# A state-space scan's decay exponents: one product with a coarse mask per head, and a triangle applied later

## The chip, the cores and the metric

The kernel runs on one NeuronCore of a Trainium2 chip. The core has a matrix engine (TensorE, "PE" in the rows, with its weight loads as "PEld"), a vector engine (VectorE, "DVE"), a scalar engine (ScalarE, "ACT"), GpSimd ("POOL") and SyncE ("SP"), which issues most transfers. Each engine works through its own list of instructions in order and waits on semaphores for the others. The metric is the device time of one execution in microseconds (us), the median over several runs.

## What is computed

The program is three transformer-like layers on 256 tokens of width 1024. The change lies in the second mixer, a state-space layer (Mamba-2 in chunks). Cut to what matters:

```
def ssd_scan(x, dt, a, bm, cm):            # 32 heads, 4 groups of 8 heads, 2 chunks of 128 tokens
    causal = np.tril(np.ones((L, L), dtype=bool))
    def step(state, inp):
        acs = jnp.cumsum(dt_k * a_g, axis=1)
        seg = acs[:, :, None] - acs[:, None, :]
        lmat = jnp.exp(jnp.where(causal, seg, -jnp.inf))     # 128 x 128 for each head
        cb = jnp.einsum("blgn,bsgn->blsg", c_k, b_k)
        w = cb[..., None] * lmat * dt_k[:, None]
        y = jnp.einsum("blsgh,bsghp->blghp", w, x_k)
        ...                                                  # plus what the state gives, and the new state
```

For each chunk and each head, a 128 x 128 matrix of decays exp(acs[l] - acs[s]) is wanted for tokens s <= l, and zero above. `a` is negative and `dt` positive, so acs falls from token to token: the exponent is at most zero where s <= l, and positive where s > l.

## The kernel before

**Weights.** All weight matrices come as a row of 1 MB chunks. SP loads a chunk into one of three buffers (`raw`); ACT rounds it to a high part (`whi`, L503) and DVE (L510), or POOL for some chunks (L518), subtracts to get the low part (`wlo`). PE multiplies each chunk three times (L522, L523, L524: input high with weight low, and so on). ACT and DVE do a chunk in two pieces of 1024 columns; "a split" below is one such piece.

**The state-space stage.** `pe_ssd_first`, `act_ssd_first` and `dve_ssd_first` make dt, the running sums (`nacs`, minus acs with tokens on partitions) and a transposed copy of the sums in a PSUM bank: 96 rows, three copies of the 32 heads, by 2 x 128 tokens. These sums are cut into three bf16 parts, so that bf16 products add up to them exactly enough: `part[0]` (ACT, L1677), `rest[0]` (DVE, L1705), `part[1]` (ACT, L1683), `rest[1]` (DVE, L1711). Then six products (`spread`, five on POOL at L1730 in `pool_ssd_parts`, one on DVE at L1713) spread them to `segs`, 96 x (2 chunks x 4 heads x 128 tokens) in bf16, with zeros where row and head don't belong together.

**The scan.** For group g (8 heads) and chunk t, `pe_seg` fills two PSUM banks, four heads each ("halves" below, h0 and h1). A half is two bf16 matmuls of 512 columns: identity by the mask `neg_sl` (-1e30 where s > l, L1829), and a one-hot selection `quad` by `segs` (L1831). There are 4 x 2 x 2 = 16 halves. `act_seg` makes E = exp(bank + nacs) by heads (L1842). `pe_ssd_scan` makes cb (L1857) and the transposes of x (L1862); `dve_ssd_scan` multiplies E by cb (L1935, "W"), x by dt (L1939, `xdt`); PE then makes y with E as weights (L1870), the state (L1877), or what the state gives (L1880, "inter"). The second half of a chunk 1 (t = 1) waits for ACT's copy of the state (L1910), and that of a chunk 0 of g > 0 for DVE's `inter` (L1959). At the end of a group y is transposed ("turn", L1891), rounded by ACT (L1925, "high") and reduced by DVE (L1979, "low").

**The order.** While the scan of group g runs, the same engines project the inputs of group g + 1, and at the end the output projection. Strings in `SSD_ORDER` say for each engine which of the streams takes its next step: `a` the scan, `b` the projections (for PE a step is half a chunk, 24 matmuls of 256 columns; later half a chunk of the output projection, 12 of 512), `T` the next split of weights. So the order of the work is fixed by hand on each engine, and an engine that waits holds all that is behind it. Decoded, PE's order around the places that matter is (p1.0a = group 1, projection 0, first half; z = the two projections of z; d0.0 = first step of the output projection):

```
head:  p0.2a p0.2b p0.0a SEG(0,0)h0 p0.0b p0.1a p0.1b SEG(0,0)h1 p1.0a p1.0b p1.1a cb(0,0) p1.1b p1.2a y(0,0) p1.2b state(0)
late:  inter(1) SEG(2,0) p3.0a p3.0b turn(1) ... cb(2,0) p3.2a y(2,0) state(2) p3.2b SEG(2,1) cb(2,1) p3.z0a p3.z0b p3.z1a p3.z1b
       y(2,1) inter(2) SEG(3,0) d0.0 d0.1 turn(2) d1.0 cb(3,0) d1.1 y(3,0) state(3) SEG(3,1) d2.0 d2.1 cb(3,1) d3.0 y(3,1)
```

A projection into a PSUM bank waits until DVE has taken the earlier content: p1.0a waits for the third convolution tap (L1577) of projection (0,0), p1.1a for that of (0,1), and d0.0 for DVE's product with z (L1800) after ACT's tanh of it.

Of the kernel before, what the change touches and what calls it, by code (L numbers as in the profile page):

```python
# [120 lines left out]
def _host_neg():  # L121
# [5 lines left out]
    out = [np.where(c > r, n, z), np.where(r > c, n, z), np.where(r % 64 <= np.arange(64)[None, :], z, n)]  # L127
# [4 lines left out]
    out.append(((a[:, None] // 4 % 8 == np.arange(8)[None, :]) & (a[:, None] < 96)).astype(np.float32))  # L132
    out.append((a[:, None] % 4 == np.arange(4)[None, :]).astype(np.float32))
# [126 lines left out]
def build(nc, wall, x_d, mem_d, cols_d, rows_d, masks_d, neg_d, out_d):  # L260
# [19 lines left out]
    with root:  # L280
# [32 lines left out]
        negf_w = 2 * 128 + 64 + 30 + 8 + 4 + 1  # L313
# [19 lines left out]
        neg_qk, neg_sl, neg_gd = negb[:, 0:128], negb[:, 128:256], negb[:, 256:320]  # L333
        quad, fourth = negb[0:96, 350:358], negb[0:96, 358:362]
# [1331 lines left out]

        def act_ssd_first(e, split):
            e.wait_ge(*at("srow", "galog"))
            e.activation(Am[:, :], srow[:, 32:64], ACTF.Exp).then_inc(*up("act.ssd", "A"))
            e.wait_ge(*at("pe.proj", C_DT))  # L1670
# [6 lines left out]
            e.activation(part[0], banks[7][0:96, 0:256], ACTF.Copy).then_inc(*up("act.ssd", "part", 0))  # L1677
# [5 lines left out]
            e.activation(part[1], rest[0], ACTF.Copy).then_inc(*up("act.ssd", "part", 1))  # L1683

        def dve_ssd_first(e, split):
# [19 lines left out]
            e.tensor_tensor(rest[0], banks[7][0:96, 0:256], part[0], SUB).then_inc(*up("dve.ssd", "rest", 0))  # L1705
# [5 lines left out]
            e.tensor_tensor(rest[1], rest[0], part[1], SUB).then_inc(*up("dve.ssd", "rest", 1))  # L1711
            e.wait_ge(*at("dve.ssd", "rest", 1))
            e.tensor_tensor(*spread(rest[1], 0, 2), MUL).then_inc(*up("dve.ssd", "segs"))  # L1713

        def spread(v, t, i):

            rows = slice(32 * i, 32 * i + 32)
            return (segs[rows, t, :, :], tl(v[rows, :], t).unsqueeze(1).to_broadcast([32, 4, 128]),
                    bc(fourth[rows, :], 128))

        def pool_ssd_parts(e):
            for t in range(2):
                for i, v in enumerate((part[0], part[1], rest[1])):
                    if (t, i) == (0, 2):
                        continue
                    if i == 2:
                        e.wait_ge(*at("dve.ssd", "rest", 1))
                    else:
                        e.wait_ge(*at("act.ssd", "part", i))
                    e.tensor_tensor(*spread(v, t, i), MUL).then_inc(*up("pool.ssd", "segs", t, i))  # L1730
                    e.wait_ge(*at("pool.ssd", "segs", t, i))
# [82 lines left out]
        def pe_seg(e, g, t):  # L1814

            for b2 in range(2):
# [6 lines left out]
                if t == 0:  # L1823
                    e.wait_ge(*at("pool.ssd", "segs", 0, 1))
                    e.wait_ge(*at("dve.ssd", "segs"))
                else:
# [68 lines left out]
        def act_ssd_scan(e, g):  # L1895
# [1207 lines left out]
```

## Time and profile before

| | us |
|---|---|
| median of 3 runs | 1207.2 (1207.15 to 1210.69) |
| the profiled execution | 1207.32 |
| its span in the trace | 1205.5 |
| PE busy | 1179.6 (98%) |
| DVE busy | 847.9 (70%) |
| ACT busy | 651.6 (54%) |
| POOL busy | 151.9 (13%) |

Busy time is the sum of an engine's instructions over the span. The state-space stage takes the span from about 360 to 560 us. A profile is read by stages: an average of 98% on PE can hide stretches in which PE stands still, and only there do the other engines set the time. Matmuls are pipelined: a row's duration is longer than the step from one start to the next, and the step is what a matmul costs in a stream.

### The profile page before, as it was taken

The page shows a single profiled execution, that of the slowest core. Times are in us where ns is not written, and L with a number is a line of the kernel's source. Part 1 is how long each engine was busy: PE and PEld are TensorE (multiplying, and loading weights), DVE is VectorE, ACT ScalarE, POOL GpSimd, SP SyncE. Part 2 cuts the span into 40 slices and gives each one's busy share as a digit, 9 for nine tenths or more (in the row PEclk, how much of TensorE's full clock was granted, in tenths as well). Part 3 has the DMA queues.
Part 4 walks back from the last instruction along what each step waited for, and adds up shares of the span by engine and source line. Part 5 has one row for each costly group of instructions (what it writes and reads, how often), then busy time and mean ns, then how long its engine had stood idle before and what let it go on. Part 6 is the DMA issues. An engine that isn't in the chain of part 4 may idle for free.

```text
span 1205.5 us, 23231 instructions
## 1 busy us (share of the span) xinstructions
PE 1179.6 (98%) x9876; PEld 1078.4 (89%) x9876; DVE 847.9 (70%) x1299; ACT 651.6 (54%) x1171; POOL 151.9 (13%) x143
## 2 busy tenths in 40 slices
PE   8999999999999999999999999999999999999998
PEld 8897789999889898978999988999989878999986
DVE  6677777888557988886788874857567776655542
ACT  4657556666446665645666653665434534644431
POOL 1320000000002332101000000103443311000000
PEclk9999999999999999999999999999999999999999
DMA  8832226565635443352755564452322322755540
GB/s 295 280 141 88 89 101 211 195 210 191 233 106 172 152 184 141 114 183 105 257 194 183 207 244 157 178 175 105 105 108 71 111 102 90 278 192 193 182 168 35
DMA packets 31623, 196.68 MB, mean 163 GB/s; under 512 B 4000, under 2 KB 5664, under 8 KB 9376
## 3 DMA queue, kind: packets, MB, share of 16 engines
q1 hardware_dynamic: 27504, 185.17, 43.3%
q10 hardware_dynamic: 4016, 10.03, 2.6%
q8 instruction: 78, 1.28, 0.4%
q14 instruction: 25, 0.20, 0.0%
HBM read 193.09 MB, written 1.05 MB: 161 GB/s over the span
## 4 chain that ended last, share of the span: by engine, by line
PE 85%; DVE 6%; ACT 4%; issue 2%; POOL 1%; DMA 1%; ACTq 1%; DVEq 0%; POOLq 0%
PE bank L522 24%; PE bank L524 23%; PE bank L523 23%; DVE wlo L510 2%; ACT whi L503 1%; PE bank L1870 1%; PE bank L1108 1%; PE bank L1165 1%; PE bank L1192 1%; PE bank L2514 1%; PE bank L702 1%; DMA raw<-in_wall 1%; PE bank L2457 1%; ACTq L973 1%; PE bank L2981 1%
## 5 line engine op out<-in xcount | busy, mean ns | idle before, releaser
L510 DVE TENSOR_TENSOR wlo<-raw,whi 128x1024 fp32r<-128x1024 f32 (+1 forms) x325 | 390.2, 1238 | 90.7 <-ACT whi L503 90.0
L522 PE MATMUL bank<-xT,wlo 128*128 128x256 f32 (+1 forms) x1512 | 425.5, 281 | 4.3 <-DVE wlo L510 2.2
L523 PE MATMUL bank<-xT,whi 128*128 128x256 f32 (+1 forms) x1512 | 419.9, 278 | 0.0
L524 PE MATMUL bank<-xT,whi 128*128 128x256 f32 (+1 forms) x1512 | 419.9, 278 | 0.0
L503 ACT ACTIVATE whi<-raw 128x1024 fp32r<-128x1024 f32 (+1 forms) x349 | 349.4, 1048 | 116.1 <-PE bank L524 86.5
L522 PEld LDWEIGHTS bank<-xT,wlo 128*128 128x128 f32 (+1 forms) x1512 | 282.2, 187 | 8.8 <-DVE xc L1577 2.8
L523 PEld LDWEIGHTS bank<-xT,whi 128*128 128x128 f32 (+1 forms) x1512 | 282.2, 187 | 0.9 <-issue 0.5
L524 PEld LDWEIGHTS bank<-xT,whi 128*128 128x128 f32 (+1 forms) x1512 | 282.0, 187 | 0.2
L644 POOL TENSOR_TENSOR rr<-rr,nhalf 128x1 f32<-128x1 f32 x34 | 24.8, 729 | 709.7 <-DVE rr L632 522.3
L522 PE MATMUL bank<-whi,gT 128*128 128x512 f32 x264 | 104.6, 396 | 0.0
L524 PE MATMUL bank<-whi,gT 128*128 128x512 f32 x264 | 104.4, 395 | 0.0
L523 PE MATMUL bank<-wlo,gT 128*128 128x512 f32 x264 | 104.3, 395 | 0.0
L522 PE MATMUL bank<-whi,xT 128*128 128x256 f32 (+1 forms) x320 | 96.0, 300 | 2.5 <-DVE xT L718 2.5
L523 PE MATMUL bank<-wlo,xT 128*128 128x256 f32 (+1 forms) x320 | 93.0, 291 | 0.0
L524 PE MATMUL bank<-whi,xT 128*128 128x256 f32 (+1 forms) x320 | 93.0, 291 | 0.0
L518 POOL TENSOR_TENSOR wlo<-raw,whi 128x1024 fp32r<-128x1024 f32 x24 | 61.3, 2559 | 120.2 <-ACT whi L503 111.5
L522 PEld LDWEIGHTS bank<-whi,xT 128*128 128x128 f32 x320 | 60.4, 189 | 7.4 <-DVE xT L718 2.8
L523 PEld LDWEIGHTS bank<-wlo,xT 128*128 128x128 f32 x320 | 60.4, 189 | 1.8 <-issue 0.5
L524 PEld LDWEIGHTS bank<-whi,xT 128*128 128x128 f32 x320 | 60.3, 188 | 1.4
L524 PEld LDWEIGHTS bank<-whi,gT 128*128 128x128 f32 x264 | 49.6, 188 | 11.9
L523 PEld LDWEIGHTS bank<-wlo,gT 128*128 128x128 f32 x264 | 49.6, 188 | 11.7
L522 PEld LDWEIGHTS bank<-whi,gT 128*128 128x128 f32 x264 | 49.6, 188 | 11.6
(383 smaller groups left out, 1747.3 us busy)
## 6 DMA issues: line engine op xcount, KB each, us to landing
raw<-in_wall SPq DMA_DIRECT2D x173, 1024.0 KB, 4.9
grow<-in_rows ACTq DMA_DIRECT2D x13, 512.0 KB, 5.8
h<-in_x SPq DMA_DIRECT2D x4, 256.0 KB, 5.1
dsk<-in_rows ACTq DMA_DIRECT2D x4, 256.0 KB, 3.5
memx<-in_mem ACTq DMA_DIRECT2D x1, 1024.0 KB, 12.1
out<-h SPq DMA_DIRECT2D x4, 256.0 KB, 2.3
masks<-in_masks SPq DMA_DIRECT2D x1, 580.0 KB, 13.4
D<-Tx ACTq DMA_DIRECT2D x4, 128.0 KB, 5.9
```

Of the source, the lines that this page charges most:

```text
L503: e.activation(whi[i % NHL][:, o:o + w], raw[i % NRAW][:, o:o + w], ACTF.Copy).then_inc(*up("act.high", p))
L510: e.tensor_tensor(wlo[i % NHL][:, o:o + w], raw[i % NRAW][:, o:o + w], whi[i % NHL][:, o:o + w], SUB).then_inc(*up("dve.low", p))
L518: e.tensor_tensor(wlo[i % NHL][:, o:o + w], raw[i % NRAW][:, o:o + w], whi[i % NHL][:, o:o + w], SUB).then_inc(*up("pool.low", p))
L522: e.matmul(out, a[1], b[0], start=start, stop=False)
L523: e.matmul(out, a[0], b[1], start=False, stop=False)
L524: return e.matmul(out, a[0], b[0], start=False, stop=stop)
L644: return e.tensor_tensor(v, v, nhalf[:, :].to_broadcast([128, n]), ALU.pow)
L702: r = e.transpose(tl(turn_bank(k, t, n), j), tl(xs_of(k, t), c), ident)
L973: e.dma_start(D2[kv][64 * l2:64 * l2 + 64, par::2, 0:256 - l2], T[kv][64 * par:64 * par + 64, :, l2:256]).then_inc(*up(f"shift{kv}", par, ...
L1108: r = e.matmul(tl(wbank(2 * m + p), i * (t + 1) + kb), qT[rows, 4 * (g // 2) + h0 + i, 128 * t:128 * t + 128], tl(kz[br][rows, g // 2, :], ...
L1165: r = e.transpose(tl(wbank(n), kb * k + i), tl(aP[place(n)], i * (W // 128) + kb), ident)
L1192: r = e.matmul(banks[6 + g // 2][64 * p:64 * p + 64, 128 * h0:128 * h0 + 128 * k], vv[br][:, kb, 64 * (g + p):64 * (g + p) + 64], aPT[(2 * ...
```

## The change

The mask and the selection go into one product. The bf16 parts of the sums stay where they are, 96 rows `parts` by 2 x 128 tokens, and the 32 rows below hold `fours`: 1 where the column's token belongs to the row's block of four tokens. The weights of a head, `pick`, hold a one-hot of the head in rows 0 to 95 and, in the 32 rows below, `later`: -1e30 where the token's block of four is later than the row's. One matmul of 128 x 128 by 128 columns then gives acs[l], and -1e30 where s lies in a later block of four than l. Within a block of four, tokens s > l are not masked: their exp is over 1. So W takes the smaller of E and 1, and multiplies by a cb that has been multiplied by a triangle of ones and zeros (`tri`).

- PE: a half is four matmuls of 128 columns in place of two of 512.
- POOL: `pool_ssd_parts` is gone. DVE: its `spread` is gone, the rests take 64 and 32 rows instead of 96.
- DVE: eight products of cb by `tri` (128 x 128 in PSUM) are new, in front of W, which becomes a scalar_tensor_tensor.
- ACT: `fours`, `later` and `pick` of group 0 ahead of dt, `pick` of the next group in each of groups 0 to 2.
- The orders of all four engines are new. PE's, decoded at the same places:

```
head:  p0.2a p0.2b p0.0a p0.0b SEG(0,0)h0 p0.1a p0.1b SEG(0,0)h1 p1.0a p1.0b p1.1a cb(0,0) p1.1b p1.2a p1.2b y(0,0) state(0)
late:  inter(1) p3.0a SEG(2,0) p3.0b turn(1) ... cb(2,0) p3.2a y(2,0) state(2) SEG(2,1) cb(2,1) p3.2b p3.z0a p3.z0b
       y(2,1) inter(2) SEG(3,0) p3.z1a p3.z1b turn(2) d0.0 cb(3,0) d0.1 y(3,0) state(3) d1.0 SEG(3,1) d1.1 cb(3,1) d2.0 d2.1 y(3,1)
```

DVE's new order has one split in place of two between the convolution of (0,2) and the first tap of (0,0), and the other after that tap.

The diff, cut:

```diff
@@ _host_neg
-    out = [np.where(c > r, n, z), np.where(r > c, n, z), np.where(r % 64 <= np.arange(64)[None, :], z, n)]
+    fours = np.where(r < 32, np.where(c // 4 == r, 1, z), np.where((r >= 96) & (c // 4 > r - 96), n, z))
+    out = [np.where(c > r, n, z), fours, np.where(r % 64 <= np.arange(64)[None, :], z, n)]
...
@@ build
-        neg_qk, neg_sl, neg_gd = negb[:, 0:128], negb[:, 128:256], negb[:, 256:320]
-        quad, fourth = negb[0:96, 350:358], negb[0:96, 358:362]
+        neg_qk, neg_gd = negb[:, 0:128], negb[:, 256:320]
+        fours, later, head1 = negb[0:32, 128:256], negb[96:128, 128:256], negb[0:96, 350:382]
...
-        segs = sb([96, 2, 4, 128], bf16, sst, "segs")
+        pick = sb([128, 8, 128], bf16, sst, "pick")
...
-        part = [stT[0:96, 128 * i:128 * i + 128].bitcast(bf16) for i in range(2)]
-        rest = [yy[1][0:96, 256 * i:256 * i + 256] for i in range(2)]
+        parts = cols[:, _COLS["fc0"][0]:_COLS["fc0"][0] + 128].bitcast(bf16)
+        rest = yy[1][0:64, 0:256]
...
+        def act_pick(e, g):
+
+            e.activation(pick[0:96, :, :], bc(head1[:, 8 * g:8 * g + 8], 128), ACTF.Copy).then_inc(*up("act.scan", "pick", g))
...
@@ act_ssd_first
             e.activation(Am[:, :], srow[:, 32:64], ACTF.Exp).then_inc(*up("act.ssd", "A"))
+            e.activation(parts[96:128, :].rearrange("p (t n) -> p t n", t=2), fours.unsqueeze(1).to_broadcast([32, 2, 128]),
+                         ACTF.Copy).then_inc(*up("act.ssd", "fours"))
+            e.activation(pick[96:128, :, :], later.unsqueeze(1).to_broadcast([32, 8, 128]), ACTF.Copy).then_inc(
+                *up("act.ssd", "later"))
+            act_pick(e, 0)
             e.wait_ge(*at("pe.proj", C_DT))
...
-            e.activation(part[0], banks[7][0:96, 0:256], ACTF.Copy).then_inc(*up("act.ssd", "part", 0))
+            e.activation(parts[0:96, :], banks[7][0:96, 0:256], ACTF.Copy).then_inc(*up("act.ssd", "part", 0))
...
-            e.activation(part[1], rest[0], ACTF.Copy).then_inc(*up("act.ssd", "part", 1))
+            e.activation(parts[0:64, :], rest, ACTF.Copy).then_inc(*up("act.ssd", "part", 1))
@@ dve_ssd_first
-            e.tensor_tensor(rest[0], banks[7][0:96, 0:256], part[0], SUB).then_inc(*up("dve.ssd", "rest", 0))
+            e.tensor_tensor(rest, banks[7][0:64, 0:256], parts[0:64, :], SUB).then_inc(*up("dve.ssd", "rest", 0))
...
-            e.tensor_tensor(rest[1], rest[0], part[1], SUB).then_inc(*up("dve.ssd", "rest", 1))
-            e.wait_ge(*at("dve.ssd", "rest", 1))
-            e.tensor_tensor(*spread(rest[1], 0, 2), MUL).then_inc(*up("dve.ssd", "segs"))
-        def spread(v, t, i):
-...
-        def pool_ssd_parts(e):
-...
+            e.tensor_tensor(parts[32:64, :], rest[32:64, :], parts[32:64, :], SUB).then_inc(*up("dve.ssd", "rest", 1))
@@ pe_seg
                 if t == 0:
-                    e.wait_ge(*at("pool.ssd", "segs", 0, 1))
-                    e.wait_ge(*at("dve.ssd", "segs"))
-                else:
-                    e.wait_ge(*at("pool.ssd", "segs", 1, 2))
-                q = 2 * g + b2
-                e.matmul(bv[:, :].rearrange("p (i n) -> p i n", i=4), identb[:, :],
-                         neg_sl.unsqueeze(1).to_broadcast([128, 4, 128]), start=True, stop=False)
-                e.matmul(bv[:, :], quad[:, q:q + 1].to_broadcast([96, 128]), segs[:, t, :, :].rearrange("p i n -> p (i n)"),
-                         start=False, stop=True).then_inc(*up("pe.scan", "seg", g, t, b2))
+                    e.wait_ge(*at("act.scan", "pick", g))
+                if (g, t) == (0, 0):
+                    e.wait_ge(*at("act.ssd", "later"))
+                    e.wait_ge(*at("act.ssd", "fours"))
+                    e.wait_ge(*at("dve.ssd", "rest", 1))
+                for i in range(4):
+                    r = e.matmul(tl(bv, i), pick[:, 4 * b2 + i, :], tl(parts, t), start=True, stop=True)
+                r.then_inc(*up("pe.scan", "seg", g, t, b2))
@@ act_ssd_scan
                 yield
+                if t and g < 3:
+                    act_pick(e, g + 1)
...
@@ dve_ssd_scan
-                e.wait_ge(*at("act.scan", "seg", g, t, 1))
-                e.wait_ge(*at("pe.scan", "cb", g, t))
-                e.tensor_tensor(E[:, :, :], E[:, :, :], banks[6][:, 0:128].unsqueeze(1).to_broadcast([128, 8, 128]),
-                                MUL).then_inc(*up("dve.scan", "w", g, t))
+
+                e.wait_ge(*at("pe.scan", "cb", g, t))
+                e.tensor_tensor(banks[6][:, 0:128], banks[6][:, 0:128], tri, MUL).then_inc(*up("dve.scan", "cb", g, t))
+                e.wait_ge(*at("act.scan", "seg", g, t, 1))
+                e.wait_ge(*at("dve.scan", "cb", g, t))
+                e.scalar_tensor_tensor(E[:, :, :], E[:, :, :], 1.0, banks[6][:, 0:128].unsqueeze(1).to_broadcast([128, 8, 128]),
+                                       ALU.min, MUL).then_inc(*up("dve.scan", "w", g, t))
...
@@ SSD_ORDER
             "pe": (
-                "bbbbbbbabbbbbbbabbbbbbbbbbbaabbbbbbababbbbbaaaaabbbaabaabbbbbbaaaabbbbbbaabaabbbbbaabaaabbaaaabbaaaabbbb"
...
+                "bbbbbbbbabbbbbbabbbbbbbbbbbaabbbbbbbaabbbbbaabaaabbaabaabbbbbbaaaabbbbbbaabaabbbbbaabbaaabaabaabaaaabbbb"
...
@@ gpsimd
             split.to(C_S + 4)
-            pool_ssd_parts(e)
```

## Rows read from the trace of the kernel before

**Rows 1.** The chain that ended last: shares of the span by engine.
```profile
PE 85%; DVE 6%; ACT 4%; issue 2%; POOL 1%; DMA 1%; ACTq 1%; DVEq 0%; POOLq 0%
```

**Rows 2.** Busy time by stretches: start:end, length, then each engine's busy us (instructions).
```profile
375.00:390.00 15.00, 13.93 (x114) 13.57 (x115) 13.83 (x19) 10.24 (x16) 7.42 (x5) 1.00 0.68 223
390.00:405.00 15.00, 12.89 (x105) 12.15 (x105) 12.88 (x22) 10.68 (x22) 3.05 (x1) 1.00 0.55 198
...
420.00:440.00 20.00, 20.00 (x164) 18.67 (x163) 16.93 (x24) 13.62 (x31) 3.36 (x5) 1.00 0.39 143
```

**Rows 3.** PE's timeline, 385 to 413: start, duration, form, [idle before, releaser].
```profile
388.10 0.36 PE L522 MATMUL bank<-xT,wlo 128*128 128x256 f32 x1 [0.27 <-DVE wlo L510]
396.35 0.39 PE L522 MATMUL bank<-xT,wlo 128*128 128x256 f32 x1 [1.91 <-DVE xc L1577]
402.47 0.39 PE L522 MATMUL bank<-xT,wlo 128*128 128x256 f32 x1 [0.20 <-DVE xc L1577]
412.17 0.33 PE L1867 MATMUL bank<-masks,bcn 128*128 128x128 f32 x1 [0.29 <-DVE E L1935]
412.77 2.00 PE L1870 MATMUL bank<-xdt,E 128*128 128x64 f32 x16 [0.27 <-DVE xdt L1939]
```

**Rows 4.** PE's timeline: two halves of the exponents and what follows.
```profile
420.98 0.39 PE L1829 MATMUL bank<-negb,identb 128*128 128x512 bf16 x1
...
421.87 0.38 PE L1857 MATMUL bank<-bcn 128*128 128x128 f32 x2
```

**Rows 5.** Weight loads of one half; and eight bf16 matmuls of 350 columns in a row.
```profile
420.98 0.10 PEld L1829 LDWEIGHTS bank<-negb,identb 128*128 128x128 bf16 x1
420.99 0.10 PEld L1831 LDWEIGHTS bank<-segs,negb 96*128 96x128 bf16 x1
...
362.27 1.35 PE L761 MATMUL bank<-negb,identb 128*128 128x350 bf16 x8
```

**Rows 6.** DVE's timeline, 377 to 390, and POOL's instructions that run beside it.
```profile
377.19 2.36 DVE L510 TENSOR_TENSOR wlo<-raw,whi 128x1024 fp32r<-128x1024 f32 x2 [0.26 <-ACT whi L503]
379.82 0.41 DVE L1705 TENSOR_TENSOR yy<-bank,stT 96x256 f32<-96x256 f32 x1
...
381.41 1.13 DVE L1711 TENSOR_TENSOR yy<-yy,stT 96x256 f32<-96x256 f32 x1
382.57 1.41 DVE L1713 TENSOR_TENSOR segs<-yy,negb 32x512 bf16<-32x512 f32 x1
384.02 3.94 DVE L510 TENSOR_TENSOR wlo<-raw,whi 128x1024 fp32r<-128x1024 f32 x2
387.88 2.42 DVE L1577 SCALAR_TENSOR_TENSOR bcn<-bank,cols,bcn 128x255 f32<-128x255 f32 x6
...
381.22 3.67 POOL L1730 TENSOR_TENSOR segs<-stT,negb 32x512 bf16<-32x512 bf16 x3 [0.78 <-ACT stT L1683]
```

**Rows 7.** PE's timeline: late waits of PE in the scan.
```profile
472.00 0.39 PE L1829 MATMUL bank<-negb,identb 128*128 128x512 bf16 x1 [0.31 <-DVE xs L1959]
520.88 0.46 PE L1857 MATMUL bank<-bcn 128*128 128x128 f32 x2 [0.30 <-DVE yT L1979]
528.00 0.39 PE L1829 MATMUL bank<-negb,identb 128*128 128x512 bf16 x1 [0.21 <-ACT stT L1910]
```

**Rows 8.** ACT's copy for dt, and PE's instruction that waits for it.
```profile
366.44 0.37 ACT L1671 ACTIVATE xs<-bank 32x256 f32<-32x256 f32 x1 [1.78 <-PE bank L524]
...
369.16 0.63 PE L571 MATMUL bank<-masks,xs 32*128 32x32 f32 x4
```

**Rows 9.** Groups by line and shape, 370 to 550: busy us, mean ns of one, idle before.
```profile
L503 ACT ACTIVATE whi<-raw 128x1024 fp32r<-128x1024 f32 x53 | 54.0, 1063 | 4.8 <-PE bank L524 3.2 <-DMA raw<-in_wall 1.4
L1935 DVE TENSOR_TENSOR E<-E,bank 128x1024 f32<-128x1024 f32 x8 | 9.7, 1217 | 2.0 <-PE bank L1857 2.0
L1979 DVE SCALAR_TENSOR_TENSOR yT<-bank,cols,yT 128x128 fp32r<-128x128 f32 x32 | 8.6, 344 | 3.0 <-ACT yT L1925 3.0
L1800 DVE SCALAR_TENSOR_TENSOR zs<-zs,bank 128x512 f32<-128x512 f32 x8 | 5.5, 686 | 5.4 <-ACT zs L1775 5.4
```

More of the change, by code:

```diff
@@ L130, in _host_neg @@
         out.append(np.where(16 * cc + 31 <= a[:, None] + 128 * t, z, n))
-    out.append(((a[:, None] // 4 % 8 == np.arange(8)[None, :]) & (a[:, None] < 96)).astype(np.float32))
-    out.append((a[:, None] % 4 == np.arange(4)[None, :]).astype(np.float32))
+    out.append(((a[:, None] % 32 == np.arange(32)[None, :]) & (a[:, None] < 96)).astype(np.float32))
     out.append((a[:, None] >= 31).astype(np.float32))
@@ L312, in build @@
         masks = sb([128, _MASKS], name="masks")
-        negf_w = 2 * 128 + 64 + 30 + 8 + 4 + 1
+        negf_w = 2 * 128 + 64 + 30 + 32 + 1
         negb = sb([128, negf_w - 1], bf16, name="negb")
@@ L1710, in dve_ssd_first @@
             e.wait_ge(*at("act.ssd", "part", 1))
-            e.tensor_tensor(rest[1], rest[0], part[1], SUB).then_inc(*up("dve.ssd", "rest", 1))
-            e.wait_ge(*at("dve.ssd", "rest", 1))
-            e.tensor_tensor(*spread(rest[1], 0, 2), MUL).then_inc(*up("dve.ssd", "segs"))
-        def spread(v, t, i):
-            rows = slice(32 * i, 32 * i + 32)
-            return (segs[rows, t, :, :], tl(v[rows, :], t).unsqueeze(1).to_broadcast([32, 4, 128]),
-                    bc(fourth[rows, :], 128))
-        def pool_ssd_parts(e):
[L1722 to L1727, printed above, removed]
-                    else:
-                        e.wait_ge(*at("act.ssd", "part", i))
-                    e.tensor_tensor(*spread(v, t, i), MUL).then_inc(*up("pool.ssd", "segs", t, i))
-                    e.wait_ge(*at("pool.ssd", "segs", t, i))
+            e.tensor_tensor(parts[32:64, :], rest[32:64, :], parts[32:64, :], SUB).then_inc(*up("dve.ssd", "rest", 1))
         def pe_ssd_proj(e, g):
@@ L1908, in act_ssd_scan @@
                     e.wait_ge(*at("pe.scan", "state", g))
-                    e.wait_ge(*(at("pe.scan", "inter", g - 1) if g else at("pool.ssd", "segs", 1, 2)))
+                    if g:
+                        e.wait_ge(*at("pe.scan", "inter", g - 1))
                     e.activation(stT[:, :], banks[5][:, :], ACTF.Copy).then_inc(*up("act.scan", "state", g))
@@ L1943, in dve_ssd_scan @@
                     e.wait_ge(*at("pe.scan", "turn", g - 1, t))
-                elif t:
-                    e.wait_ge(*at("pool.ssd", "segs", 1, 2))
                 e.tensor_tensor(yy[t][:, :], banks[7][:, :], dsk[:, :], MUL).then_inc(*up("dve.scan", "skip", g, t))
@@ L2763, in build @@
             "pe": (
[L2764 to L2765 removed]
+                "bbbbbbbbabbbbbbabbbbbbbbbbbaabbbbbbbaabbbbbaabaaabbaabaabbbbbbaaaabbbbbbaabaabbbbbaabbaaabaabaabaaaabbbb"
+                "bbaabbbbbaaaaaaabbbbbbbaaaabbaaaabbaabaabaabaaabbbaabbbbaaaabbTTTTTTTTTTTTTTTTTTTTTTTTTTTTTTTTTTTTTTTTTT"
                 "TTTTTTTT"),
             "act": (
[L2768 to L2769 removed]
+                "TTbbbTbbbTbbbTaTbbbbbbTTabbbTbbbbbbTTbbbaaTTaTabbbbbbTaaaabbbbbTTbbaaTTTaaaaabbbaabbbTbbbaaTTTaabbbbbbaa"
+                "aabbbTaabbTTbbTaaaaabbbTaaaabbbTTTTbbbaTaaaaabbbaaTbbbTaaaaabbbbbbbaaTTTaaTaaTaaaaTTTTaaaaaTTTaaTTbbbbbb"
                 "bbbbbbbb"),
             "dve": (
[L2772 to L2773 removed]
+                "TTbbbbbbTbbbbTbbTTbbbbbbTTbbbbbbaaaabbbbTTTababTbbbbaaabbaaabbbbTTTaTTTTaaaTbbbbaababaaabbbbbabaaabbbbbT"
+                "TTbaaTbbbbaaTTTaaaTbbbbaabbaTTTaaaTabbbbTaaabbaaaTbbbbabaaaTbaabbbbaTaaaTaTaaaTTTTaaTaTaaTTaaTTaTTbbbbbb"
                 "bbbbbbbb"),
             "pool": (
[L2776 removed]
+                "TTTTTTTTTTTTTTaaaaaaaaaaTTTaaaaaaaTTTTTaaaaaaaaaaTTTTaaaaaaaTTTTaaaaaaaaaaaaaaaaaaaaaaaaaaaaaaaaTTTTTTTT"
                 "TTTTTTTTTTTTaa"),
```

7 lines of the change are left out of this document (removed).

## The prediction

> **What bounds the kernel now.** I read the chain of work that ended last first: PE carries 85% of the span [rows 1]. So a microsecond taken from PE's stream is worth nearly a microsecond, and other engines count only where PE stands still. The busy times by stretches say where that is [rows 2]: from 420 us on PE is busy 20.00 of 20.00 us, but only 13.93 of 15.00 from 375 and 12.89 of 15.00 from 390, where the scan starts. There DVE is busy 13.83 and 12.88. PE's timeline names what ended each pause there: DVE every time, 0.27, 1.91, 0.20, 0.29 and 0.27 us, 2.94 together [rows 3]. A restart after a pause also shows its first matmul longer than its neighbours and starts late in the stream, by about 0.16 us each (a row's end lies about that much behind the start of the next one in a stream); with five restarts the pauses cost some 3.7 us. DVE's list tells why it is late: between 381 and 388 it does the two last steps of the three-part cut (1.13 and 1.41) and a pair of weight splits that takes 3.94, while POOL runs its spreads; a like pair took 2.36 shortly before [rows 6]. So the change touches two things that set the time: PE's own columns, and DVE's lateness at the head.
>
> **Term A, the matmuls.** A half goes from two matmuls of 512 columns to four of 128. Two halves in the trace take 0.89 us from the start of the first to the start of the next work [rows 4]: 0.445 a half. For the new ones the trace has bf16 matmuls of 350 columns with a weight load each: eight in 1.35, the last one lasting about 0.31, so 1.04 / 7 = 0.149 each [rows 5]; by columns 128 would take 0.054. I take 0.057, so 0.23 a half, a gain of 0.215, and 16 x 0.215 = 3.4 us. What speaks against it is that there are now four weight loads where there were two. A load's row lasts 0.10 us, longer than 128 columns. But two loads start 0.01 us apart [rows 5], so most of that row is latency that the next load overlaps. Bounds: a load that takes its whole row, 4 x 0.098 = 0.39 a half, leaves 16 x 0.055 = 0.9 us; loads that are hidden without any overhead give 16 x (0.445 - 0.214) = 3.7. I am near the upper end, because the pair of loads in row 5 is the same kind of load.
>
> The Trainium skill ("TensorE: Matmul & The Clock Gate", section "Back-to-back issue gap") gives about 81 ns for each 128-column matmul in a stream of load and matmul pairs. By that figure (an estimate from the page) a half takes 0.32, the term is 16 x 0.12 = 1.9, and the kernel comes out at 1202.8. No row here has bf16 matmuls of just 128 columns, so the trace neither agrees nor disagrees.
>
> **Term B, the head.** DVE loses the spread (1.41), and without POOL's spreads beside it I take the last cut at the 0.41 of the first one, 0.7 less, and the pair of splits at 2.36, 1.6 less [rows 6]. Together 3.7: DVE begins the convolution of (0,2) at about 384.3 instead of 388. Follow PE: before, p0.0b let go at 388.10 - 0.27 - 0.16 = 387.67 [rows 3]; a half that is 0.215 shorter makes it 387.45, the splits of p0.1 are long done, so the 0.27 pause goes. p0.1 takes 396.35 - 2.07 - 0.445 - 388.10 = 5.7 us [rows 3], to 393.1, and the second half ends at 393.3. p1.0a then waits for the third tap of (0,0). With the new order DVE does the six taps of (0,2) in 2.4 [rows 6] to 386.75, its silu, one split, the first tap at about 389.3 (PE's p0.0b and ACT's 1 us come before), a second split, and the other taps to about 392.9. PE need not wait: 393.3 instead of 396.35. p1.1a needs the taps of (0,1), by the same counting at 398.9 against PE's 399.0, a tie. y(0,0) now has one projection step more in front (p1.2b, half of 5.7), which covers W. So all five pauses could go, 3.7 us. I take the first two in full (2.18 + 0.32 = 2.5) and half of the other three (0.6), because the tie can tip: 3.1 us. Bounds: 0, if a weight transfer or ACT holds PE there instead, and 3.7.
>
> **Term C, the new order later on.** SEG(2,0) now has a projection step in front of it, and the 0.31 pause for DVE goes (0.47 in the stream); SEG(3,1) likewise, 0.21 (0.37) [rows 7]. But SEG(2,1) now stands right behind state(2), as SEG(3,1) did before, and pays that 0.37 plus the 0.2 by which its first half has become shorter; SEG(3,0), which still stands right behind inter(2), hides 0.2 less. And d0.0, now right behind p3.z1b and turn(2), must wait until ACT has made the tanh of z (half of an L503 piece, 0.53) and DVE the product (0.69) [rows 9]; the transposes of the turn cover most of that, about 0.7 stays open (0.3 to 1.2); turn's rounding is then covered by d0.0, and the 0.30 pause of cb(3,0) [rows 7] mostly goes. In sum +0.84 - 0.57 - 0.2 - 0.7 + 0.2, about -0.5 us, bounds -1.5 and +0.5.
>
> **What I cost at nothing.** ACT's `fours`, `later` and `pick` of group 0 stand in front of the copy for dt: one short and two of 1024 columns, about 0.4 + 2 x 1.06 by L503 [rows 9] = 2.5. ACT waits there for 1.78 us anyway, so dt comes 0.7 later, at 367.5; its only reader on PE starts at 369.16 [rows 8]. If that cover were gone it would cost 0.7. The three later picks, 1.06 each, lie where ACT waits for PE; behind them are queued tanhs and splits, and PE's next halves need them only a group later. Should one fall in front of a late exp, it costs 1.06. cb by `tri`, eight times, is like L1979 (0.344) [rows 9]. DVE now waits for cb before it waits for E; behind it are queued W, xdt and the splits. Where cb comes long before E it is hidden; where cb comes last (after the "low" of the last group), W ends 0.35 later, and y has a step of 2.8 us in front of it, of which W and xdt used 1.9. W itself as scalar_tensor_tensor stays as it is: L1800 is of that kind and takes 0.686 for 512 columns, L1935 1.217 for 1024 [rows 9]. A dearer W is bounded by twice that, but no row speaks for it. The transfers of weights follow DVE's splits, which come earlier.
>
> **Sum.** 3.4 + 3.1 - 0.5 = 6.0 us. The profiled execution took 1207.32 (span 1205.5 and 1.8 around it), and the median of the runs is 1207.2, 0.1 from it: 1207.3 - 6.0 = 1201.3 us.
>
> **Rivals.** (1) *The head stays as late as it is.* Term B is 0: PE stands at p1.0a or p1.1a for something that was hidden behind DVE, a transfer or the chain PE, ACT, DVE through one bank and its three taps. For it: the tie at p1.1a. Against it: every pause in rows 3 names DVE, and DVE is 92% busy there. Time: 1207.3 - 3.4 + 0.5 = 1204.4. (2) *The weight loads show.* Term A is 0.9: 1207.3 - 0.9 - 3.1 + 0.5 = 1203.8. For it: the load's 0.10 us row against 0.054 of columns; against it: loads 0.01 apart. (3) *Both*: 1206.9. (4) *Slower: DVE becomes the bound in the scan.* The places are cb to y of (1,0), (1,1), (2,0) and (3,0), where PE now has a single step, 2.8 us, between them. DVE's chain there is 0.35 + 1.22 + 0.69 = 2.3 from cb. It decides once DVE reaches cb more than 0.5 late; DVE is busy 16.93 of 20 [rows 2] and the new order puts splits (1.2 each) between. Two splits late, 2.4, costs 1.9 at each of the four, 7.6 in all: 1207.3 - 6.0 + 7.6 = 1208.9. Against it: PE had pauses of at most 0.5 there before, and the splits can be counted in the order: at most one stands directly ahead.
>
> **How the numbers follow.** The forecast has 0.55 (1199.9 to 1203.2 by the bounds of A, B and C that I think likely), rival 1 0.17, rival 2 0.12, rival 3 0.07, rival 4 0.09. The predicted time is the forecast's. The range must leave out no more than 2 in 10: it runs from 1199.8 (A and B at their upper ends, C at zero: 1207.3 - 3.7 - 3.7 = 1199.9) to 1206.6, which takes in rivals 1 and 2 and leaves out 3 and 4 and a little below. A measurement of this kernel can tell about 0.3%, 3.6 us, from no change, so "faster" is below 1203.6 and "slower" above 1210.8: faster is the forecast, half of rival 2 and a little of rival 1, 0.63; slower is the upper half of rival 4, 0.06; the same is the rest, 0.31.
>
> **What would show it.** In the profile of the changed kernel: a half's four matmuls 0.05 to 0.06 apart and the next work 0.23 behind the first (A; 0.32 or 0.39 means that loads show). The pair of splits behind the cut at 2.4 instead of 3.94, no pause of PE above 0.5 us between 376 and 415, and p1.0a at about 393 instead of 396.35 (B). A pause of 0.4 to 1.2 in front of d0.0, and one of about 0.6 between the halves of SEG(2,1) (C). ACT's copy for dt at about 367 with PE's turn of it unmoved. Wrong would be: pauses in front of y that name E or xdt, or PE waiting for weights at the head.

## The result and the profile after

The changed kernel takes 1228.2 us (median of 4 runs, 1227.0 to 1229.6) against 1207.3 of the kernel before, measured beside it: a ratio of 1.0171, interval 1.0155 to 1.0186. The forecast was 1201.3 and its range ended at 1206.6, so it was wrong by its sign. The profiled execution took 1227.2, with a span of 1225.1 against 1205.5.

The page of the changed kernel, busy time by engine, and the shares of the chain that ended last (before in [rows 1]):

```profile
PE 1200.4 (98%) x9908; PEld 1103.1 (90%) x9908; DVE 845.7 (69%) x1306; ACT 657.5 (54%) x1177; POOL 141.4 (12%) x138
...
PE 90%; DVE 5%; ACT 2%; issue 2%; POOL 1%; DMA 0%; DVEq 0%; POOLq 0%; ACTq 0%
```

PE's share of the chain has grown from 85% to 90%, and its busy time by 20.8 us. So the time isn't in a new wait; PE's own instructions have become slower. The stretch that the change aimed at looks as forecast at first sight (busy time by stretches, columns as in [rows 2]; the same work stands some 7 us later than before, dt's turn at 376.32 instead of 369.16):

```profile
375.00:390.00 15.00, 14.25 (x118) 13.86 (x117) 9.26 (x18) 10.57 (x16) 0.00 (x0) 1.00 0.44 151
390.00:405.00 15.00, 15.00 (x131) 14.91 (x130) 13.58 (x24) 12.09 (x23) 0.00 (x0) 1.00 0.67 241
420.00:440.00 20.00, 19.59 (x161) 18.48 (x161) 17.27 (x29) 14.02 (x25) 7.70 (x5) 1.00 0.40 155
```

From 390 PE is busy 15.00 of 15.00; before, with the work 7 us earlier, it was 12.89 [rows 2]. So I went through the trace by stages, from the start of one known product to that of another. In the rows xT is the transposed input of a projection, gT the transposed inner values of a feed-forward block and yT the transposed result of the state-space layer, each kept as a high and a low part. The up-projection of the first feed-forward block, from the last turn of its norm (L825, L827 after) to the first product with gT, before and then after:

```profile
188.71 0.60 PE L825 MATMUL bank<-masks,xs 128*128 128x128 f32 x4
...
292.51 0.40 PE L522 MATMUL bank<-whi,gT 128*128 128x512 f32 x1
```
```profile
189.49 0.60 PE L827 MATMUL bank<-masks,xs 128*128 128x128 f32 x4
...
299.36 0.40 PE L524 MATMUL bank<-whi,gT 128*128 128x512 f32 x1
```

That is 103.80 before and 109.87 after, in code that the change doesn't touch. The state-space stage, from the turn of dt (369.16, [rows 8]) to the last product with yT, got shorter. Its end before, then its start and end after:

```profile
566.80 0.39 PE L524 MATMUL bank<-whi,yT 128*128 128x512 f32 x1
```
```profile
376.32 0.29 PE L573 MATMUL bank<-masks,xs 32*128 32x32 f32 x1
...
571.16 0.39 PE L526 MATMUL bank<-whi,yT 128*128 128x512 f32 x1
```

197.64 has become 194.84. All stages, worked out in this way, make up the difference of the spans:

| stage | before, us | after, us | difference |
|---|---|---|---|
| up to the first up-projection | 188.71 | 189.49 | +0.8 |
| three up-projections | 103.8 each | 109.87 each | +18.2 |
| state-space stage | 197.64 | 194.84 | -2.8 |
| between the second and the third (memory, third mixer, a down-projection) | 342.78 | 345.50 | +2.7 |
| all the rest | | | +0.6 |
| span | 1205.5 | 1225.1 | +19.5 |

Within an up-projection PE never pauses. Windows of PE alone (length, PE busy, instructions, granted clock, DMA share, GB/s), the same 50 us before and then after:

```profile
200.00:250.00 50.00, 50.00 (x443) 1.00 0.59 203
```
```profile
200.00:250.00 50.00, 50.00 (x419) 1.00 0.60 208
```

The clock is full in both, and the transfers bring as much. But 443 products have become 419 (each count has some two that only reach into the window). From start to start, over the products that begin in it, a step takes 113.3 ns before and 120.0 after. A product's own row still lasts 0.28; only the step to the next one has grown.

### The profile page after: what moved, and what is told of

It is laid out like the page before. It is cut to its first block, busy times and chain, and to the rows that moved or that the text cites. A ratio compares the mean times of both kernels' runs of the same rounds, so it can differ in the third digit from the quotient of the medians.

```text
span 1225.1 us, 23298 instructions
## 1 busy us (share of the span) xinstructions
PE 1200.4 (98%) x9908; PEld 1103.1 (90%) x9908; DVE 845.7 (69%) x1306; ACT 657.5 (54%) x1177; POOL 141.4 (12%) x138
## 3 DMA queue, kind: packets, MB, share of 16 engines
HBM read 193.10 MB, written 1.05 MB: 158 GB/s over the span
## 4 chain that ended last, share of the span: by engine, by line
PE 90%; DVE 5%; ACT 2%; issue 2%; POOL 1%; DMA 0%; DVEq 0%; POOLq 0%; ACTq 0%
PE bank L524 25%; PE bank L526 24%; PE bank L525 24%; DVE wlo L512 2%; PE bank L1110 1%; PE bank L1860 1%; PE bank L1167 1%; PE bank L1194 1%; PE bank L704 1%; DVE xc L1579 1%; ACT whi L505 1%; PE bank L2508 1%; PE bank L2451 1%; PE bank L2974 0%; DVE xT L720 0%
## 5 line engine op out<-in xcount | busy, mean ns | idle before, releaser
L524 PE MATMUL bank<-xT,wlo 128*128 128x256 f32 (+1 forms) x1512 | 432.1, 286 | 1.6 <-DVE wlo L512 1.6
L526 PE MATMUL bank<-xT,whi 128*128 128x256 f32 (+1 forms) x1512 | 427.7, 283 | 0.0
L525 PE MATMUL bank<-xT,whi 128*128 128x256 f32 (+1 forms) x1512 | 424.9, 281 | 0.0
```

Of the source, the lines that this page charges most:

```text
L524: e.matmul(out, a[1], b[0], start=start, stop=False)
L525: e.matmul(out, a[0], b[1], start=False, stop=False)
L526: return e.matmul(out, a[0], b[0], start=False, stop=stop)
```

## The experiments

Two theories. **P**: the step depends on where the operands lie. The wider mask (`negf_w`, 363 to 383 columns) makes `negb` longer, and every tensor allocated behind it moves by 32 bytes on each partition: xT from 128960 to 128992, gT, yT and the rest alike. **Q**: the instructions of the change cost the time. Unused bytes in the allocation part the two. Addresses below are the program's own; "distance" is that of xT from `whi` and `wlo`, beyond a multiple of 256 bytes: 64 before, 96 after.

**Moved without the change, changed without the move.** The four edits, in this order: the changed kernel with 32 bytes more (all behind `negb` 64 further than before), the kernel before with the 32 bytes of the change, with 32 in front of xT and 32 behind it, and with 64.

```
  e1, behind negb (changed kernel):  +  sb([128, 8], name="pad")
  e2, behind negb (kernel before):   +  sb([128, 8], name="pad")
  e3, ahead of and behind xT:        +  sb([128, 8], name="pad")   (twice)
  e4, behind negb (kernel before):   +  sb([128, 16], name="pad")
```

> The changed kernel with 32 unused bytes behind the mask tensor, so that every tensor behind it starts at a multiple of 64 bytes again. Theory P (place in memory: the wider mask tensor moved xT and all behind it by 32 bytes, and TensorE's products that read xT became slower): each up-projection takes 103.8 us again instead of 109.9, matmul steps 113 ns instead of 119 to 122, and the kernel comes out at 1202 to 1204, since the state-space stage alone had become 2.8 us shorter. Theory Q (the change itself costs the 21 us, by another way than memory): 1226 to 1230 as before the padding.

> The kernel before with 32 unused bytes behind the mask tensor and nothing else: its tensors get the addresses that they have in the changed kernel. Theory P: 1207.3 + 3 x 6.07 for the three up-projections + about 4 for the other products of xT = 1229 to 1232. Theory Q: 1207, no change.

> The kernel before with 32 unused bytes in front of xT and 32 behind it: only xT lies 32 bytes off a multiple of 64, all else stands at multiples of 64. Theory P with xT as the one operand that matters: as when all is shifted, 1229 to 1232. Rival P2 (the products are slowed by another of the shifted tensors, or by the engines that read and write the others): 1207 to 1212. Theory Q: 1207.

> The kernel before with 64 unused bytes behind the mask tensor: all addresses behind it are those of the changed kernel with its padding, at multiples of 64 (xT at a multiple of 512 instead of 64 only). Theory P with 64 bytes as what counts: 1207, no change. Rival P3 (a coarser multiple counts too): 1203 or less. Theory Q: 1207.

| run | xT's distance | us | ratio to before | products in 50 us, by up-projection |
|---|---|---|---|---|
| e1, changed | 128 | 1220.5 | 1.0095 [1.0071, 1.0119] | 424, 424, 424 |
| e2, before | 96 | 1231.5 | 1.0189 [1.0163, 1.0215] | 419, 419, 419 |
| e3, before | 96 | 1226.3 | 1.0145 [1.0123, 1.0167] | 419, 419, 419 |
| e4, before | 128 | 1222.8 | 1.0118 [1.0096, 1.0141] | 419, 424, 419 |

The window from 200 to 250 us in e2 (443 products before, 419 in the changed kernel):

```profile
200.00:250.00 50.00, 50.00 (x419) 1.00 0.59 208
```

The kernel before, not changed in any instruction, loses 24 us by 32 unused bytes, and its count falls to that of the changed kernel. Q falls. At the same addresses the changed kernel is the faster one: 1228.2 against 1231.5 (e2), and 1220.5 (e1) against 1222.8 (e4). What also fell is the first form of P, that a multiple of 64 bytes mends it: e1 and e4 lie on one and are still slow. e3 and e2 differ by 5 us with xT at the same place and the same counts, so other tensors' places count too. And in e4 the stages of one execution differ: at 128 a stage goes at 120.0 ns or at 118.7.

**Which distance.** e5 is the changed kernel with `nhalf` in a spare column of `valid`, so that h, xT and all behind them get their old addresses; e6 and e8 move by 128; e7 moves raw, whi and wlo along with xT.

```
  e5:  -  valid = sb([128, 2], name="valid")
       +  valid3 = sb([128, 3], name="valid")
       +  valid = valid3[:, 0:2]
       -  nhalf = sb([128, 1], name="nhalf")
       +  nhalf = valid3[:, 2:3]
  e6, behind negb (changed kernel):  +  sb([128, 24], name="pad")
  e7, ahead of raw (kernel before):  +  sb([128, 16], name="pad")
  e8, behind negb (kernel before):   +  sb([128, 32], name="pad")
```

> The changed kernel whole, with its columns packed so that h, xT and every tensor behind them lie at the addresses that they have in the kernel before (xT at 128960); only four small tensors stay 32 bytes further. Theory P, the places of the tensors in SBUF set the step of the matmuls: the products of xT with whi step 113 ns again in the up-projections (119 in the changed kernel), the up-projection stage takes 103.8 us again, and what is left is the change's own gain, so 1207.5 - 3 to 5 = 1202 to 1204.5 us, the candidate that beats both kernels. Theory Q, the change's own instructions cost the time: about 1228 us, steps of 119 ns.

> The changed kernel with 96 unused bytes behind negb, so that all that lies behind it is 128 bytes further than in the kernel before (xT at 129088). Theory P with a pattern that repeats every 128 bytes: as with the places kept, 1202 to 1204.5 us and steps of 113 ns. Theory P without such a pattern (what counts is something finer or a distance): 1218 to 1230 us and steps of 118 to 122 ns. Theory Q: about 1228 us.

> The kernel before with 64 unused bytes ahead of raw, so that raw, whi, wlo and everything behind them move together: xT lies at 129024 as in the run with 64 bytes behind negb, but its distance to whi is the one of the kernel before. If the distance between xT and the weights sets the step: 1207 us and 113 ns. If xT's own place sets it: about 1222 us and 119 to 121 ns, as in that run.

> The kernel before with 128 unused bytes behind negb (xT at 129088, the same places as in the changed kernel with 96 bytes). A pattern that repeats every 128 bytes: 1207 us, steps of 113 ns. None: 1215 to 1232 us. The difference to the changed kernel at the same places is the change's own gain, 2 to 4 us by theory P, 0 or less by theory Q.

e5: 1205.2, ratio 0.9991 [0.9970, 1.0013]. e6: 1199.2, 0.9923 [0.9903, 0.9944]. e7: 1207.1, 1.0000 [0.9989, 1.0011]. e8: 1203.1, 0.9959 [0.9942, 0.9977]. The same window in e5, then in e7:

```profile
200.00:250.00 50.00, 50.00 (x443) 1.00 0.57 200
```
```profile
200.00:250.00 50.00, 50.00 (x443) 1.00 0.57 200
```

With its old addresses back, the changed kernel has 443 products again. In e7 xT lies where it lay in e4, 64 bytes further, and there are 443: not xT's address counts but its distance to the weights. The three up-projections of one execution of e6, 128 bytes further:

```profile
200.00:250.00 50.00, 50.00 (x427) 1.00 0.55 190
600.00:650.00 50.00, 50.00 (x444) 1.00 0.53 190
1045.00:1095.00 50.00, 50.00 (x443) 1.00 0.54 189
```

At a distance of 192 a whole stage goes at 117.8 or at 113.3 ns, 4 us apart, with everything at the same place. At 64 both paces occur too: e10 below, at 64, has 427, 443 and 443. So e6 can't tell whether the pattern repeats at 128 bytes; e14 below does, where 96 and 224 differ. In no trace does the pace change within an up-projection: it is the same from its first 48 products on to its last. The runs of e6 and e8, and of others at 64 and 192, come in groups about 4 us apart, as stages at one pace or the other would make them. None of the experiments explains what chooses. With the two kernels at the same places, e6 is 3.8 us faster than e8, as much as the change gains in e5 (below).

**Which pair, which period, and what the order gave back.** e9 is e6 with two steps of DVE's order moved; e10 moves whi, wlo and xT against raw; e11 moves wlo and xT against whi; e12 is the changed kernel moved by 256 bytes.

```
  e9, DVE's order:  -  "...aaaabbbbTTTabab..."  "...aaaTbbbbaabba..."
                    +  "...aaaabbbabTTTbab..."  "...aaaTbbbaabbba..."
  e10, ahead of whi (kernel before):  +  sb([128, 16], name="pad")
  e11, ahead of wlo (kernel before):  +  sb([128, 16], name="pad")
  e12, behind negb (changed kernel):  +  sb([128, 56], name="pad")
```

> The changed kernel with 96 unused bytes (1199.2 us), and two steps of DVE's order moved: the rounding of y(1,1) ahead of the second tap of p3.0, and the skip of y(0,0) with xde ahead of the second tap of p1.1. If the order written out for the change is what gives part of the gain back (term C), PE's pause in front of the second turn falls from 1.98 to about 0.7 us (the square root on POOL is ready at 474.7), the pause in front of the first state from 1.00 to 0.2 or less, and the time comes to 1199.2 - 2 = about 1197 us. If those pauses only wait for something else, or the taps that are pushed back take their place, it stays at 1199 us.

> The kernel before with 64 unused bytes between raw and whi: whi, wlo and all behind them move together, raw stays. If only the distance between the two operands of the products (xT and the weights) counts: 1207 us and steps of 113 ns, as when raw moved too. If the distance between the operands and raw, which the transfers write meanwhile, counts: 1215 to 1230 us and steps of 118 to 122 ns.

> The kernel before with 64 unused bytes between whi and wlo: wlo and all behind it move, whi stays, so xT keeps its distance to wlo and loses the one to whi. If a product's step is set by the distance of xT to the weights loaded for the next product: the products beside which whi is loaded (two of three: xT by wlo, and the first xT by whi) step by about 120 ns, and the third, beside which wlo is loaded, by 113; some 1215 to 1222 us. If the distance to the weights in use counts: xT by wlo 113 ns, xT by whi 120. If the distance to both counts alike, or to neither: all three alike.

> The changed kernel with 224 unused bytes behind negb, so that all behind it is 256 bytes further than in the kernel before. A pattern that repeats every 256 bytes: as with the places kept, steps of 113 ns in the up-projections and 1202 to 1205 us. One that repeats every 128 bytes only: as with 96 unused bytes, 117.5 ns and 1199 us. Neither: other steps, between 1197 and 1230 us.

e10 takes 1207.4, ratio 1.0000 [0.9985, 1.0015]: raw's place doesn't count. e11 takes 1226.5, 1.0150 [1.0126, 1.0174], with 419 products in the window. The distance to wlo alone, left as it was, saves nothing: the three products of a round step by 118.9, 121.1 and 120.0 ns (means of some 260 starts), and the forecast that one of them keeps 113 fell. e11 also moves wlo against whi; no run parts that from xT's distance to whi. e12 takes 1204.0, 0.9976 [0.9954, 0.9998], with 444 products: 256 bytes further all is as with the old addresses.

e9 takes 1202.5, where e6 took 1199.2, with runs from 1194.5 to 1203.0; two of its up-projections went at 117.8 ns in the profile where one of e6 did, so the total decides nothing. Its state-space stage does: 191.86 us against 193.10 of e6, 1.24 less. PE's wait in front of the second turn, in e5 (as in e6) and then in e9:

```profile
475.56 0.33 PE L1882 MATMUL bank<-masks,yy 128*128 128x128 f32 x1 [1.98 <-DVE yy L1968]
```
```profile
475.79 0.65 PE L1882 MATMUL bank<-masks,yy 128*128 128x128 f32 x4 [0.85 <-DVE yy L1968]
```

And e5's DVE in front of it:

```profile
474.24 0.87 DVE L1580 SCALAR_TENSOR_TENSOR xc<-bank,cols,xc 128x255 f32<-128x255 f32 x2 [2.00 <-ACT xc L1567]
475.03 0.48 DVE L1968 TENSOR_SCALAR yy<-yy,rr 128x512 f32<-128x512 f32 x1
```

L1968, which the expectation calls a rounding, is the product of y with the scale of its norm (`rr`), and PE waits for it. It stood behind two taps that themselves waited 2.00 us for ACT. With the step moved ahead of them PE's wait is 1.1 us shorter. The pause in front of the first state went too (e9's PE is busy 15.00 of 15.00 from 405 to 420), but one of 0.61 in front of y(0,1) came.

**Moving one pair and not the other.** e13 is e5 with e9's order and 128 unused bytes between the group of xT and the room that gT, yT and the third mixer's ygT share; e15 is the kernel before with the same 128 bytes and nothing else.

```
  e13, e15, ahead of "boot = ExitStack()":  +  sb([128, 32], name="pad")
```

> The changed kernel with h and xT at the places of the kernel before (as in the run with the places kept, 1205.2 us), the two moved steps of DVE's order, and 128 unused bytes between these tensors and gT, yT and the others that each stage lays over the same room. If the step of a product follows from the distance of its own two operands, products of xT in the up-projections keep 113 ns while those of gT fall from 234 to 227 ns, as in the run 128 bytes further: 3 x 264 x 6.5 ns = 5.1 us, and about 1 for yT; the moved steps take 1.2; so 1205.2 - 7 = about 1198 us. If the whole layout counts and not the pair, the steps of xT or of gT change otherwise, and the time lies between 1200 and 1215.

> The kernel before with 128 unused bytes between xT's group of tensors and gT, yT and the others that are laid over the same room: nothing of the change. If the pair of operands counts: products of gT step by 227 ns instead of 234, of xT by 113 as before, 1207.2 - 6 = about 1201 us. If the layout as a whole counts: other steps, 1200 to 1215 us.

e13 takes 1200.9, ratio 0.9943 [0.9924, 0.9962], e15 1205.2, 0.9979 [0.9963, 0.9996]. The first down-projection, products of gT (loaded) with streaming weights, before and in e13:

```profile
300.00:350.00 50.00, 50.00 (x216) 1.00 0.53 190
```
```profile
300.00:350.00 50.00, 50.00 (x222) 1.00 0.53 187
```

In e13 and e15 those with whi step by 227.3 to 227.5 ns where the kernel before and e5 have 233.8, while xT keeps its two paces of 64, so each pair goes by its own distance. Both totals lie above the forecasts (1198 and 1201). In the profiles some up-projections went at 117.8 ns, which would make up for that: one of three in e13's, two in e15's (an execution of 1209.4). e13, with the same unused bytes as e15, leads it by 4.4 us, the share of the change and of e9's two moves. e6 and e13 both beat both kernels, by 0.6 to 0.8% against the kernel before.

**Two reads of TensorE, or others beside them.** In e14 and e16 PE runs nothing but streams of such products. In e14 each distance has 192 products alone, and later as many with splits and transfers beside them; in e16 there are 32 streams that begin anew after a pause. Neither computes the layers. The products, condensed:

```
  e14:  + e.matmul(out, b, xhi[:, c + x:c + 256 + x], ...)   # c = 0, 8, ... 56 columns (0 to 224 bytes)
        + e.matmul(out, a, xlo[:, c + x:c + 256 + x], ...)
        + e.matmul(out, a, xhi[:, c + x:c + 256 + x], ...)
  e16:  + e.wait_ge(S["act"], i + 1)                        # a pause, then the same with c = 16, 24, 0 or 48
```

> A kernel that computes none of the reference (its output is its input): products like those of the up-projections, 192 for each of eight distances between moving operand and weights (0, 32, ... 224 bytes beyond a multiple of 256), first with TensorE alone, then once more with ACT and DVE making splits and transfers writing other tensors beside it. Theory: TensorE's own reads of the two operands disturb each other, so the step depends on the distance with nothing beside it: 113 ns at 64, 117 at 192, 119 to 122 at 0, 32, 96 and 128. Rival: only writes of other engines and transfers beside the products make the difference: all eight alike (107 to 113 ns) alone, and different in the second part. Second rival: neither shows it, and it comes from something else in the kernel (which buffers take turns).

> A kernel that computes none of the reference (its output is its input): TensorE alone, 32 streams of 96 products like those of the up-projections, each begun anew after a short pause of varied length; 16 streams at a distance of 64 bytes beyond a multiple of 256 (8 with one pair of weight buffers, 8 with two that take turns), 8 each at 96, 0 and 192. Theory: a stream settles into its pace when it begins, and at 64 there are two paces; so some streams at 64 step by 113 ns and others by 117.7, none at 96 or 0 goes below 117, and 192 is like 64. First rival: the pace of 113 needs buffers that take turns; then only those 8 of the 16 show it. Second rival: neither, all streams at 64 step by 117.7, and the 113 of the whole kernel comes from something that these streams lack.

Windows of PE in e14, alone, at 0, 32, 64, 96, 128, 160, 192 and 224 bytes, in this order:

```profile
40.00:60.00 20.00, 20.00 (x169) 1.00 0.00 1
62.00:82.00 20.00, 20.00 (x173) 1.00 0.00 1
85.00:105.00 20.00, 20.00 (x172) 1.00 0.00 1
108.00:128.00 20.00, 20.00 (x169) 1.00 0.00 1
131.00:151.00 20.00, 20.00 (x170) 1.00 0.00 1
153.00:173.00 20.00, 20.00 (x173) 1.00 0.00 1
176.00:196.00 20.00, 20.00 (x172) 1.00 0.00 1
199.00:219.00 20.00, 20.00 (x172) 1.00 0.00 1
```

The same with other work beside them (32, 96 and 192 bytes; busy time of PE, weight loads, DVE, ACT and POOL, as in [rows 2]). The transfers had ended by the last, the splits of DVE and ACT had not:

```profile
250.00:270.00 20.00, 20.00 (x172) 20.00 (x171) 20.00 (x19) 20.00 (x22) 0.00 (x0) 1.00 0.96 384
...
295.00:315.00 20.00, 20.00 (x169) 20.00 (x168) 20.00 (x18) 20.00 (x22) 0.00 (x0) 1.00 0.95 374
...
364.00:384.00 20.00, 20.00 (x173) 20.00 (x172) 20.00 (x19) 20.00 (x22) 0.00 (x0) 1.00 0.01 2
```

By the starts, TensorE alone steps by 120.0 ns at 0 and at 96, 118.7 at 128 and 117.3 to 118.3 at the others, and the writes beside it change nothing, neither splits on both engines nor, while they ran, transfers of 384 GB/s. So TensorE needs nothing beside it to show the difference, and the rival of the writers falls. That its two reads, of the moving operand and of the weights, disturb each other is the reading that fits; no run here looks inside. The Trainium skill ("TensorE: Matmul & The Clock Gate", section "Step-by-step: what each phase is for") says that two independent read ports serve the moving operand and the weight load, so that loading weights takes no read bandwidth from the running product. By that all eight distances would step alike; the rows differ. The 113 ns did not show in e14 at 64. In e16 (streams at 64, at 64 with buffers taking turns, at 96, at 0, and two at 192):

```profile
47.00:57.00 10.00, 10.00 (x87) 1.00 0.00 0
146.00:156.00 10.00, 10.00 (x87) 1.00 0.00 0
246.00:256.00 10.00, 10.00 (x85) 1.00 0.00 0
347.00:357.00 10.00, 10.00 (x86) 1.00 0.00 0
448.00:458.00 10.00, 10.00 (x90) 1.00 0.00 0
532.00:542.00 10.00, 10.00 (x90) 1.00 0.00 0
```

All 16 streams at 64 step by 117.8 ns, all 8 at 96 and all 8 at 0 by 119.9 to 120.0, all 8 at 192 by 113.3 once under way. So TensorE alone has the pace of 113 as well. Beginning anew after a pause changed the pace of no distance, and the pace of 113 doesn't need buffers that take turns: theory and first rival both fell. The second rival held for the streams at 64, but not in its reason, since these streams do reach 113 at 192. What decides between 113.3 and 117.8 at 64 and 192 stays open. No run here has the pace of 113 at 0, 96 or 128.

## Why the prediction was wrong

**What the profile showed before** was read rightly: PE bounds the kernel, and a microsecond of its stream is one of the time. The step that failed is the sum, 1207.3 - 6.0: it puts all that lies outside the terms A, B and C at nothing, without a reason. Every product was taken at its old duration, and the wider constant moved its operands: +18.2 us in the up-projections, +4.1 elsewhere outside the state-space stage, and 1.0 inside it (194.84 against 193.85 in e5, which has the old places). In e5 all of this is gone: its span is 1201.3, 4.2 below the kernel before. A step "what does a longer tensor move?" with the price of e2 (24 us) would have carried the whole sign. No row of the kernel before has that price, but the diff shows the longer tensor (columns 350 to 382 of `negb`, which ended at 362). None of the four rivals contained it, and rival 4, the only slower one (1208.9), is another mechanism; it did not come.

Against e5 the terms can be judged. The state-space stage goes from 197.64 to 193.85 us:

```profile
368.71 0.29 PE L574 MATMUL bank<-masks,xs 32*128 32x32 f32 x1
...
562.56 0.40 PE L527 MATMUL bank<-whi,yT 128*128 128x512 f32 x1
```

3.8 us gained, where 6.0 were forecast.

**Term A held, a little smaller.** Two halves in e5, and what follows:

```profile
417.31 0.62 PE L1822 MATMUL bank<-cols,pick 128*128 128x128 bf16 x8
417.74 0.36 PE L525 MATMUL bank<-whi,xT 128*128 128x256 f32 x1
417.94 0.28 PE L526 MATMUL bank<-wlo,xT 128*128 128x256 f32 x1
```

The eight matmuls are 0.43 / 8 = 0.054 apart, as foreseen, and their loads don't show (rival 2 falls). The Trainium skill ("TensorE: Matmul & The Clock Gate", section "Back-to-back issue gap") gives about 81 ns for each such pair of load and matmul; by that, an estimate, the eight would take 0.65, and the rows disagree. But the first product behind them steps by 0.20 instead of 0.115, which the prediction didn't have. From 417.31 to 417.94 less one product is 0.515 for two halves, 0.257 each instead of 0.23. Before it was 0.445 [rows 4], so 16 x 0.19 = 3.0 us instead of 3.4.

**Term B held.** In e5 the last cut takes 0.41, the pair of splits behind it 2.36, and the taps of (0,2) begin at 384.06 (forecast 384.3):

```profile
381.07 0.41 DVE L1723 TENSOR_TENSOR cols<-yy,cols 32x256 bf16<-32x256 f32 x1
381.78 2.36 DVE L513 TENSOR_TENSOR wlo<-raw,whi 128x1024 fp32r<-128x1024 f32 x2 [0.29 <-ACT whi L506]
384.06 2.43 DVE L1580 SCALAR_TENSOR_TENSOR bcn<-bank,cols,bcn 128x255 f32<-128x255 f32 x6
```

All five pauses of [rows 3], 2.94 us, are gone; one in front of the first state came:

```profile
413.65 0.67 PE L1868 MATMUL bank<-xs,Bt 128*128 128x512 f32 x1 [0.91 <-DVE xs L1945]
```

So 2.0 us of pauses and four restarts at 0.16: about 2.7 of the 3.1. Rivals 1 and 3 fall.

**Term C was sized wrongly.** Its own terms add to -0.43, which the prediction rounds to -0.5. The later pauses in e5, besides the turn's 1.98 shown above:

```profile
488.81 0.29 PE L1822 MATMUL bank<-cols,pick 128*128 128x128 bf16 x2 [0.42 <-ACT stT L1904]
501.73 0.29 PE L1822 MATMUL bank<-cols,pick 128*128 128x128 bf16 x2 [0.52 <-DVE xs L1954]
509.06 0.50 PE L525 MATMUL bank<-whi,yT 128*128 128x512 f32 x1 [0.53 <-DVE zs L1792]
```

The three that I named (SEG(2,1), SEG(3,0), d0.0) came at the sizes given, and those of [rows 7] went. The turn of group 1, at which I hadn't looked, went from 0.37 to 1.98. All later pauses make 3.45 against 1.50 before, with a restart less: -1.8 instead of -0.5. e9 shows it as part of the change's new order, not of the arithmetic. 3.0 + 2.7 - 1.8 = 3.9, against 3.8 measured in the stage.

**At nothing** I had ACT's three extra steps ahead of the copy for dt. It holds: in the changed kernel that copy starts at 374.25, and PE's turn of dt is set by the products ahead of it.

```profile
373.29 1.05 ACT L1671 ACTIVATE pick<-negb 96x1024 bf16<-96x1024 bf16 x1
374.25 0.36 ACT L1682 ACTIVATE xs<-bank 32x256 f32<-32x256 f32 x1
```

W stays at its cost too (1221 ns after, 1217 before [rows 9]):

```profile
L1931 DVE SCALAR_TENSOR_TENSOR E<-E,bank 128x1024 f32<-128x1024 f32 x8 | 9.8, 1221 | 0.7
```

Had the tensors kept their places, the forecast's own account with A, B and C at their measured sizes would have given 1207.3 - 3.9 = 1203.4. e5's profiled execution took 1203.4. Its runs, from 1203.4 to 1213.2, have their median at 1205.2, so the figure itself agrees partly by luck: it is one execution with all three up-projections at 113.3 ns.

## What to carry to other kernels

Before costing what a change does, list what it moves: a constant that grows by 20 columns shifts every tensor allocated behind it, and this kernel, which its products bound, went 24 us slower (e2) or 4 us faster (e8) by such a shift alone. Compare a changed kernel with one that has the old instructions at the new addresses, or put the new bytes where nothing moves; otherwise the places are measured and not the change. When a span grows while waits shrink, count instructions per window in a stage that the change leaves alone.

## What the hardware showed that I had not expected

The step of a 128x256 product in a gapless stream at full granted clock (1.00) depends on the distance between its moving operand and its weights in SBUF: 113.3, 117.3 to 118.7 or 120.0 ns, with a pattern that came back at 256 bytes in e12 and did not depend on writes beside it (e14). Products of 512 columns show it too (227 or 234 ns for gT). In the same layout a stage can run at 113.3 or at 117.8 ns (64 and 192 bytes), or at 118.7 or 120.0 (128 bytes, e4), and it keeps its pace to its end; what chooses is not known. Nor is the whole pattern settled: e16 gives 113.3 at 192 where e14, whose tensors lie otherwise beyond the 256 bytes, gives 117.8.
